# One layer of a gated hybrid decoder: the first products of the second token half in another order on TensorE

## The reference

```python
h = rms_norm(x, mix_norm)
z = h @ w_in            # 1024 columns in, 6696 out, split among four mixers and four gates
# A: indexer (iq, ik, iw) picks keys, attention over them; B: causal pooling
# C: chunked spatial gating; D: stick-breaking attention
merged = sum_n sigmoid(gate_n) * (o_n @ w_branch[n])
x = x + merged @ w_out
h = rms_norm(x, ffn_norm)
x = x + (silu(h @ w_gate) * (h @ w_up)) @ w_down
```

## Time and profile before

| | |
|---|---|
| median of three runs | 753.76 us |
| the profiled execution, its own time | 753.66 us |
| its span | 751.9 us |
| TensorE (PE) busy | 746.8 us, 99% of the span |
| VectorE (DVE) busy | 613.8 us, 82% |
| ScalarE (ACT) busy | 413.5 us, 55% |
| GpSimd (POOL) busy | 123.7 us, 16% |
| mean granted TensorE clock | 1.000 |

### The profile page before, as it was taken

How to read it: one execution, slowest core, us unless ns; L and a number is a source line. 1 busy time by engine, 2 the same in 40 slices (tenths; PEclk the granted TensorE clock), 3 DMA queues, 4 the chain that set the end, 5 groups by cost and what they waited for, 6 DMA issues and landing times.

```text
span 751.9 us, 11619 instructions
## 1 busy us (share of the span) xinstructions
PE 746.8 (99%) x4542; PEld 661.6 (88%) x4542; DVE 613.8 (82%) x835; ACT 413.5 (55%) x639; POOL 123.7 (16%) x140
## 2 busy tenths in 40 slices
PE   8999999999999999999999999999999999999998
PEld 8988888988888888779888899999889999999887
DVE  6645988878788976695999899889989888888991
ACT  6654545456663655465449656556544556656430
POOL 6200050457303121741330000000000000000000
PEclk9999999999999999999999999999999999999999
DMA  8381213231133223415526635335073333339202
GB/s 282 102 243 43 70 57 113 64 105 57 57 112 102 67 71 98 165 59 171 138 98 172 179 117 164 114 110 199 4 259 108 111 112 111 113 112 324 69 29 84
DMA packets 67878, 89.55 MB, mean 119 GB/s; under 512 B 3108, under 2 KB 52592, under 8 KB 67696
## 3 DMA queue, kind: packets, MB, share of 16 engines
q1 hardware_dynamic: 65696, 84.55, 34.6%
q0 software_dynamic: 1984, 4.14, 2.8%
q10 hardware_dynamic: 144, 0.13, 0.1%
HBM read 81.99 MB, written 4.19 MB: 115 GB/s over the span
## 4 chain that ended last, share of the span: by engine, by line
PE 98%; DMA 1%; DVE 0%; ACT 0%; issue 0%; SPq 0%; DVEq 0%
PE bank L2531 14%; PE bank L2532 14%; PE bank L2533 14%; PE bank L2862 9%; PE bank L2861 9%; PE bank L2863 9%; PE bank L3044 5%; PE bank L3048 5%; PE bank L3046 5%; PE bank L2954 2%; PE bank L2955 2%; PE bank L2956 2%; PE bank L2986 1%; PE bank L2987 1%; PE bank L2985 1%; PE bank L2746 1%
## 5 line engine op out<-in xcount | busy, mean ns | idle before, releaser
L2531 PE MATMUL bank<-h_hi,w_hi 128*128 128x512 f32 (+1 forms) x336 | 128.5, 382 | 0.0
L2533 PE MATMUL bank<-h_hi,w_lo 128*128 128x512 f32 (+1 forms) x336 | 127.5, 379 | 0.0
L2532 PE MATMUL bank<-h_lo,w_hi 128*128 128x512 f32 (+1 forms) x336 | 127.4, 379 | 0.0
L2861 PE MATMUL bank<-t_hi,w_hi 128*128 128x256 f32 x320 | 88.4, 276 | 0.0
L2863 PE MATMUL bank<-t_hi,w_lo 128*128 128x256 f32 x320 | 88.3, 276 | 0.0
L2862 PE MATMUL bank<-t_lo,w_hi 128*128 128x256 f32 x320 | 88.3, 276 | 0.0
L1647 DVE TENSOR_TENSOR w_lo<-raw,w_hi 128x2048 fp32r<-128x2048 f32 x26 | 62.8, 2417 | 14.0 <-ACT w_hi L983 12.5
L2533 PEld LDWEIGHTS bank<-h_hi,w_lo 128*128 128x128 f32 x336 | 63.2, 188 | 12.1
L2531 PEld LDWEIGHTS bank<-h_hi,w_hi 128*128 128x128 f32 x336 | 63.2, 188 | 11.9 <-issue 0.3
L2532 PEld LDWEIGHTS bank<-h_lo,w_hi 128*128 128x128 f32 x336 | 63.2, 188 | 11.4
L2862 PE MATMUL bank<-f_lo,w_hi 128*128 128x256 f32 x240 | 66.3, 276 | 0.0
(11 more groups left out here) (419 smaller groups left out, 1918.8 us busy)
## 6 DMA issues: line engine op xcount, KB each, us to landing
raw<-in_w_in_dram SPq DMA_DIRECT2D x26, 1024.0 KB, 5.1
raw<-in_w_ffn_up_dram SPq DMA_DIRECT2D x11, 1024.0 KB, 5.2
raw<-in_w_ffn_gate_dram SPq DMA_DIRECT2D x10, 1024.0 KB, 5.1
raw<-in_w_ffn_down_dram SPq DMA_DIRECT2D x7, 1024.0 KB, 5.1
raw<-in_w_branch_dram SPq DMA_DIRECT2D x4, 1024.0 KB, 4.9
b<-in_w_ffn_down_dram SPq DMA_DIRECT2D x4, 1024.0 KB, 6.4
x_sb<-in_x_dram SPq DMA_DIRECT2D x6, 512.0 KB, 4.7
o<-in_w_out_dram SPq DMA_DIRECT2D x2, 1024.0 KB, 7.3
```

The lines of the kernel that those rows point to most:

```text
L2531: mm(dst, l_hi, r_hi, start=start, stop=False)
L2532: mm(dst, l_hi, r_lo, start=False, stop=False)
L2533: return mm(dst, l_lo, r_hi, start=False, stop=stop)
L2861: mm(dst, l_hi, r_hi, start=begin and k == 0, stop=False, skip_group_check=True)
```

## The change

Only the order of TensorE's instructions in `first_chunks` changes; no instruction is added or taken away, and the order on ScalarE, VectorE and SyncE is the same. Half 0 keeps its products, without transposes among the last of them. Then the five transpose groups of half 1 stand in one batch. Then for each k the step of chunk 0 is followed at once by the step of chunk 1, j = 0, and j = 1 comes at the end by itself.

```diff
--- before.py
+++ after.py
@@ -2631,40 +2631,52 @@
                     turn_h(0, k)
                 pe.wait_ge(S["first_hi"], 1)
                 pe.wait_ge(S["first_lo"], 1)
-                for half in range(2):
+
+                def first_product(half, k):
                     cols = slice(half * SEQ // 2, (half + 1) * SEQ // 2)
-                    for k in range(KT):
-                        pe.wait_ge(S["h_lo_ready"], half * KT + k + 1)
-                        if k + 5 < KT:
-                            turn_h(half, k + 5)
-                        if half == 0 and k == KT // 2:
-                            pe.wait_ge(hi_ready, 1)
-                            pe.wait_ge(lo_ready, 1)
-                        w = w_hi[:, k * P:(k + 1) * P]
-                        mm(bank[0][:, cols], w, h_hi[:, k, cols], start=k == 0, stop=False)
-                        last = mm(bank[0][:, cols], w, h_lo[:, k, cols], start=False, stop=k == KT - 1)
-                    if half:
-                        last.then_inc(filled, 1)
-                    for j in range(MT):
-                        for k in range(KT):
-                            if half == 0 and j == 0:
-                                for piece, (a, z) in enumerate(SECOND_LOWS):
-                                    if a == k and z < KT:
-                                        pe.wait_ge(S["second_hi"], (z + 1) // 2)
-                                        pe.wait_ge(S["second_lo"], piece + 1)
-                                    elif a == k:
-                                        pe.wait_ge(hi_ready, 2)
-                                        pe.wait_ge(lo_ready, 2)
-                            w = slice(w_at(1) + k * CW + j * P, w_at(1) + k * CW + (j + 1) * P)
-                            last = three(bank[1 + j][:, cols], w_hi[:, w], w_lo[:, w], h_hi[:, k, cols], h_lo[:, k, cols],
-                                         k == 0, k == KT - 1)
-
-                            if (half, j) == (0, 1) and k >= KT - 4:
-                                turn_h(1, k - KT + 4)
-                                if k == KT - 1:
-                                    turn_h(1, 4)
-                        if half:
-                            last.then_inc(filled, 1)
+                    w = w_hi[:, k * P:(k + 1) * P]
+                    mm(bank[0][:, cols], w, h_hi[:, k, cols], start=k == 0, stop=False)
+                    return mm(bank[0][:, cols], w, h_lo[:, k, cols], start=False, stop=k == KT - 1)
+
+                def second_product(half, j, k):
+                    cols = slice(half * SEQ // 2, (half + 1) * SEQ // 2)
+                    w = slice(w_at(1) + k * CW + j * P, w_at(1) + k * CW + (j + 1) * P)
+                    return three(bank[1 + j][:, cols], w_hi[:, w], w_lo[:, w], h_hi[:, k, cols], h_lo[:, k, cols],
+                                 k == 0, k == KT - 1)
+
+                for k in range(KT):
+                    pe.wait_ge(S["h_lo_ready"], k + 1)
+                    if k + 5 < KT:
+                        turn_h(0, k + 5)
+                    if k == KT // 2:
+                        pe.wait_ge(hi_ready, 1)
+                        pe.wait_ge(lo_ready, 1)
+                    first_product(0, k)
+                for k in range(KT):
+                    for piece, (a, z) in enumerate(SECOND_LOWS):
+                        if a == k and z < KT:
+                            pe.wait_ge(S["second_hi"], (z + 1) // 2)
+                            pe.wait_ge(S["second_lo"], piece + 1)
+                        elif a == k:
+                            pe.wait_ge(hi_ready, 2)
+                            pe.wait_ge(lo_ready, 2)
+                    second_product(0, 0, k)
+                for k in range(KT):
+                    second_product(0, 1, k)
+                for k in range(5):
+                    turn_h(1, k)
+                for k in range(KT):
+                    pe.wait_ge(S["h_lo_ready"], KT + k + 1)
+                    if k + 5 < KT:
+                        turn_h(1, k + 5)
+                    first = first_product(1, k)
+                    if k == KT - 1:
+                        first.then_inc(filled, 1)
+                    last = second_product(1, 0, k)
+                last.then_inc(filled, 1)
+                for k in range(KT):
+                    last = second_product(1, 1, k)
+                last.then_inc(filled, 1)
 
             first_chunks()
```

## The result

The changed kernel takes 757.26 us in the median of six runs (755.26 to 757.58), the kernel before 753.69 us (753.31 to 754.41): a ratio of 1.0042, with a 95% interval of 1.003 to 1.0055. That is slower, as forecast, but by 3.57 us, where 1.8 us were forecast (755.5), and outside the range of 754.7 to 756.3. The six runs are of two kinds, and the granted clock tells them apart: five have 0.998 in the mean over the span and take 756.7 to 757.6 us, one has 1.000 and takes 755.26.

The account below looks back on a forecast made before the run. TensorE, 99% busy, was taken as the bound, with VectorE's chain level with it near 30.78 us. The chain's +1.79 us, instead of TensorE's own +0.12, gave 755.5 us (+0.24%), range 754.7 to 756.3.

Parts of the forecast that it names:

- TensorE by itself: TensorE's own reordered work up to the transposes of ws: ends at 30.01 instead of 29.89 us, +0.12 us.
- The new stall: TensorE idle ahead of transpose group 5, until the first h_lo of half 1 frees its bank: about 0.5 us.
- The chain: ScalarE's splits, then VectorE's low parts, ikw and iq_lo, delay TensorE's product of chunks 2 and 3 by 1.79 us.
- ScalarE's gap: ScalarE stands still 1.1 us before the split of chunk 3, until TensorE finishes chunk 0 at 26.93 us.
- the late h_hi: ScalarE's last h_hi of half 1 follows later transposes, so its split of chunk 2 starts 1.10 us later.
- the wait for chunk 0: ScalarE's split of chunk 3 must wait until TensorE finishes chunk 0; previously covered by 0.48 us.
- Does it last: After the product of chunks 2 and 3, TensorE waits for nothing new and keeps the 1.79 us delay to the end.
- The clock: Rival: TensorE's idle time of some 1.7 us around 31 us drops its clock, 1.5 us more, 757.1 us; 5%.
- twice the gap: Assumed length of slow clock after TensorE's idle time: some 3 us, half of it lost, 1.5 us more.
- The wait for chunk 0 costs nothing: Rival: ScalarE splits chunk 3 right behind chunk 2, leaving only 1.10 us of delay, 754.9 us; 10%.
- TensorE doesn't wait for iq_lo: Rival: TensorE's own order sets the start of chunks 2 and 3; no slower, perhaps faster, 753.4 to 753.9 us; 4%.
- The indexer waits: Rival: late iq_lo parts land behind 43.6 us and delay the indexer's products, 756 to 757.5 us; 3%.

Follow-up runs that it names:

- own place: Changed kernel, but chunk 0's split weights in separate memory, so ScalarE's split of chunk 3 need not wait for chunk 0; 755.04 us, ratio 1.0012.
- five fillers: Changed kernel with five transposes of the identity added in TensorE's wait for ikw; 755.63 us, ratio 1.0024.
- pairs with own place: Kernel before, with only chunk 0's steps paired with chunk 1, j = 0, transposes unmoved, and chunk 0's split weights in separate memory; 754.72 us, ratio 1.0009.
- two extra instructions: Kernel before, TensorE's order untouched, with two added VectorE instructions ahead of ikw; 754.68 us, ratio 1.0011.
- pairs alone: Kernel before, with only chunk 0's steps paired with chunk 1, j = 0, transposes where they stood; 756.67 us, ratio 1.003.
- VectorE late: Kernel before, TensorE's order untouched, with four added VectorE instructions ahead of ikw; 756.35 us, ratio 1.0033.
- the changed kernel again: The changed kernel unaltered, measured in a second series against the kernel before; 757.02 us, ratio 1.0034.

## Why the prediction was right in its sum and wrong in its time

**TensorE by itself, +0.12.** It held. Counted from L1687, the batch was forecast 1.96 behind it and came 1.95 (20.62 - 18.67); the transposes of ws came at 11.86, forecast 11.87. The new stall was some 0.45 us by the starts, from about 21.73, where ten transposes in starts of 0.11 end, to 22.18; the row counts 0.30 of it as idle.

**The chain, +1.79.** It held: +1.82. ScalarE's gap, forecast 1.1, was 1.02; ikw came 13.04 behind L1687, forecast 13.01; the product 14.46, forecast 14.43. The experiments show that both parts of it are as said: the late h_hi, forecast 1.10 and measured 1.08, and the wait for chunk 0, the rest, forecast 0.69 and measured 0.74.

**Does it last.** It held. No wait of TensorE behind it is new, and the changed kernel's runs without the fall of the clock, 755.26 to 755.45 us, are 1.5 to 1.6 us above the kernel before and next to the 755.5 that the sum gave.

**The clock, 5%.** This is the step that failed: the sum has nothing for a fall of the clock behind the new gap, and the fall, given 5%, is what happens in nine of twelve runs of the changed kernel and costs some 1.6 us. Its place was on the list, and nearly its price (757.1 forecast, 757.26 measured). That the price came so close is partly luck: no row stood behind the 3 us of slow clock ("twice the gap"), and in the four traces with a fall the slow stretch is 3.4 us long. The argument against it was that TensorE had idled for up to 1.6 us without a fall. That wait stands at the very start, and the transposes behind it run at half pace, so it said nothing of what an idle time of that length does to an engine that already runs at the full clock; the two others were 0.4 us long. Kernels with 1.2 to 1.3 and 0.3 us of idle time in their traces had the fall in nine of twelve, four of seven and two of five runs. Those with 0.4 to 0.5 and 0.3 us (own place, five fillers, pairs with own place, two extra instructions) had it in none of 42. The idle times are read from one trace of each series. The rule of the Trainium skill that was named there (TensorE: Matmul & The Clock Gate, section "Why this matters for your kernels"), that idle gaps between bursts of matmuls bring the clock back to half, agrees with this in its kind. It warns of longer gaps than these, though, and here the measurement decides: shorter ones were enough.

**The rivals.** The wait for chunk 0 costs nothing: refuted by the own place. TensorE doesn't wait for iq_lo: refuted by VectorE's two extra instructions. The indexer waits: no such wait appears.

## What to carry to other kernels

An operation that is moved later on the engine that sets the end can be free there and still cost: look on each other engine for what waits on the moved instruction, here a weight split that overwrites what the product reads, and follow that chain back. Where the list of waits shows no wait, two engines can still be level with each other; two extra instructions on the other engine tell. And where TensorE is to idle as long as here, 1.2 us and 0.3 more, price the fall of its clock as the likely case; five transposes of the identity in the wait took it out.

## What the runs showed of the hardware that was not expected

The fall of the clock differs from run to run of one program: nine of twelve runs of the changed kernel, four of seven with the pairs alone and two of five with VectorE late had it. What decides it isn't shown: the four traces, with 1.2 to 1.3 and 0.3 us of idle time, are all of runs with the fall, and that the idle time was as long in the others is only likely by their times. It comes behind the idle time, not in it, and not at one distance: the granted clock falls 0.1 us (pairs alone), 0.7 us (VectorE late), 1.2 us (the changed kernel again) and 1.3 us (its first trace) behind the start of the product. In all four traces it is then 0.50 for 3.4 us and back at 1.00. That takes about 1.6 us more by the traces; between the medians of the runs with and without it lie 1.3 to 2.3 us in the four series.

The start of the kernel varies by up to 0.8 us between profiled runs of any kernel here (L1687 at 17.91 to 18.72), as much as half of what was to be measured.
